# Writing a table of bias rows to DRAM in 21 small transfers, one at a time, in place of two large ones

## What is computed

```
bias = tab_gr[g6, r6, t5_bucket(dist)]          # first block, 8 heads (NSA)
s = einsum(q, k) * scale + bias
...
logits = logits + bias_table[t5_bucket_2(t - s)] # second block, 12 heads of three kinds
```

## Time and profile before

| | |
|---|---|
| median of three runs | 2925.42 us |
| the profiled execution's own time | 2927.45 us |
| its span (first to last instruction) | 2925.6 us |
| PE busy | 2827.9 us (97%) |
| DVE busy | 1870.2 us (64%) |
| ACT busy | 1250.5 us (43%) |
| POOL busy | 154.5 us (5%) |
| weight blocks (raw<-wstream) | 470, 4.8 us from issue to landing in the median |
| the two writes of bias rows | 2 MB and 3.25 MB, 45.9 and 45.8 us to landing |

### The profile page before, as it was taken

One profiled execution on the slowest core, in us unless ns is written; L12 is line 12 of the kernel. 1 busy time (PEld: TensorE's weight loads), 2 busy tenths in 40 slices (PEclk: granted clock), 3 DMA queues, 4 the chain that ended last, 5 costly groups with the idle time before them and its releaser, 6 DMA issues.

```text
span 2925.6 us, 43772 instructions
## 1 busy us (share of the span) xinstructions
PE 2827.9 (97%) x17530; PEld 2518.4 (86%) x17530; DVE 1870.2 (64%) x1955; ACT 1250.5 (43%) x1159; POOL 154.5 (5%) x125
## 2 busy tenths in 40 slices
PE   7898899999999999999999999999999999999997
PEld 5777788888889988888888999988888888888986
DVE  7554555567755678877777545575555765657576
ACT  4343445653363444544444333343334343434442
POOL 3000000000000001000000000010000000000330
PEclk9999899999999999999999999999999999999999
DMA  6546444445545655555555555555554466555753
GB/s 206 194 160 187 152 148 151 160 173 179 178 158 203 243 200 188 179 185 183 186 186 186 218 185 190 185 190 186 186 185 163 174 208 205 184 194 198 281 211 129
DMA packets 94811, 545.51 MB, mean 186 GB/s; under 512 B 11528, under 2 KB 25992, under 8 KB 34288
## 3 DMA queue, kind: packets, MB, share of 16 engines
q1 hardware_dynamic: 84768, 511.01, 49.4%
q0 software_dynamic: 9936, 32.92, 4.0%
HBM read 519.44 MB, written 24.38 MB: 186 GB/s over the span
## 4 chain that ended last, share of the span: by engine, by line
PE 91%; DVE 3%; DMA 3%; ACT 2%; issue 0%; POOL 0%; DVEq 0%; SPq 0%; ACTq 0%
PE gemm L527 46%; PE gemm L530 23%; PE mix L520 3%; PE mix L522 3%; PE mix L521 3%; DMA raw<-wstream 3%; PE gemm L521 2%; PE gemm L522 2%; PE gemm L520 2%; PE mix L527 1%; PE mix L787 1%; DVE wlo L1407 1%; PE mix L627 1%; PE mix L530 1%; ACT whi L970 0%
## 5 line engine op out<-in xcount | busy, mean ns | idle before, releaser
L527 PE MATMUL gemm<-HX,whi 128*128 128x512 f32 x5728 | 2027.6, 401 | 30.2 <-issue 12.3
L530 PE MATMUL gemm<-HX,wlo 128*128 128x256 f32 x5728 | 1555.1, 282 | 0.0
L970 ACT ACTIVATE whi<-raw 128x2048 fp32r<-128x2048 f32 x470 | 899.3, 1914 | 1416.3 <-DMA raw<-wstream 1413.7
L1407 DVE TENSOR_TENSOR wlo<-raw,whi 128x2048 fp32r<-128x2048 f32 x470 | 1086.0, 2311 | 384.5 <-ACT whi L970 383.7
L527 PEld LDWEIGHTS gemm<-HX,whi 128*128 128x128 f32 x5728 | 1066.6, 189 | 266.8 <-issue 25.3
L530 PEld LDWEIGHTS gemm<-HX,wlo 128*128 128x128 f32 x5728 | 1089.2, 190 | 29.8 <-issue 0.7
L1432 DVE TENSOR_REDUCE arena<-gemm 128x256 f32<-128x512 f32 (+1 forms) x173 | 119.6, 691 | 314.7 <-PE gemm L527 314.6
L520 PE MATMUL mix<-ACTH,whi 128*128 (+1 forms) x528 | 149.7, 284 | 0.0
L522 PE MATMUL mix<-ACTH,wlo 128*128 (+1 forms) x528 | 149.7, 283 | 0.0
L521 PE MATMUL mix<-ACTL,whi 128*128 (+1 forms) x528 | 149.7, 283 | 0.0
L522 PE MATMUL gemm<-OH,wlo 128*128 128x256 f32 x384 | 108.9, 284 | 0.0
(11 more groups left out here) (354 smaller groups left out, 2544.6 us busy)
## 6 DMA issues: line engine op xcount, KB each, us to landing
raw<-wstream SPq DMA_DIRECT2D x470, 1024.0 KB, 4.8
scratch<-gate_scratch POOLq DMA_DIRECT2D x12, 512.0 KB, 5.1
gate_scratch<-scratch SPq DMA_DIRECT2D x32, 128.0 KB, 4.6
GL<-gate_scratch POOLq DMA_DIRECT2D x8, 512.0 KB, 5.3
gate_scratch<-arena SPq DMA_DIRECT2D x32, 128.0 KB, 4.6
bias_scratch<-arena POOLq DMA_DIRECT2D x1, 3328.0 KB, 45.8
btile<-bias_scratch POOLq DMA_DIRECT2D x21, 128.0 KB, 2.4
XT<-xT SPq DMA_DIRECT2D x4, 512.0 KB, 9.2
```

What stands on the lines that cost most here:

```text
L527: return pe.matmul(bank.rearrange("p (c t) -> p c t", c=2), whi[slot][:, w], mx, start=first, stop=last)
L530: return pe.matmul(bank[:, 0:T], wlo[slot][:, w], mh, start=False, stop=False)
L970: f(whi[slot][:, :], raw[slot][:, :], ACT.Copy).then_inc(s["hi_ready"], 1)
L1407: tt(wlo[slot][:, :], raw[slot][:, :], whi[slot][:, :].bitcast(F32), ALU.subtract).then_inc(s["lo_ready"], 1)
```

## The change

The two large writes are replaced by a loop over all 21 rows, ahead of the first read. Each turn issues one transfer that writes one row's first `SEG` = 384 columns 128 times over (196,608 bytes), and waits until it has landed. The waits for the second write go, or count to 21 transfers.

```diff
@@ -405,12 +405,10 @@
             pool.wait_ge(s["bias_evac"], 1)
 
-            def rows_out(a, b):
-                pool.dma_start(bias_d[a:b, :, 0:ROWW], brow[a:b, :].unsqueeze(1).to_broadcast([b - a, P, ROWW])
+            for row in range(N_BROW):
+                pool.dma_start(bias_d[row:row + 1, :, 0:SEG], brow[row:row + 1, 0:SEG].unsqueeze(1).to_broadcast([1, P, SEG])
                                ).then_inc(s["bias_out"], 16)
-
-            rows_out(0, HEADS)
-            pool.wait_ge(s["bias_out"], 16)
+                pool.wait_ge(s["bias_out"], 16 * (row + 1))
 
...
                 bias(h, h)
-                if h == 2:
-                    rows_out(HEADS, N_BROW)
 
...
             pool.wait_ge(s["nsa_logit"], HEADS)
-            pool.wait_ge(s["bias_out"], 32)
             pool.wait_ge(s["f_taps"], N_UP)
...
-            act.wait_ge(s["bias_out"], 32)
+            act.wait_ge(s["bias_out"], 16 * N_BROW)
```

## The result

The changed kernel takes 2897.89 us in the median of four runs (2895.51 to 2898.79), the kernel before in the same series 2925.43 us. The ratio is 0.9907, with a 95% interval of 0.9893 to 0.9921. The forecast was 2936 us, with a range of 2885 to 2966: the time lies in the range, but the sign was wrong.

What follows compares the result with a forecast made beforehand. PE was taken as the bound, with two weight-block stalls worth 39.2 us. A loop of 21 turns at 11.6 us ending at 294.3 us gave +10.2 us: 2937.6, less 2.0 to the median, rounded to 2936 us, range 2885 to 2966.

Steps and rivals of the forecast that it cites:

- What bounds it: PE, busy 97% of the span, stalls twice on weight blocks delayed by the two row writes: 14.0 and 25.2 us.
- C: Time of one turn of POOL's row-write loop (issue, transfer, wait): 11.6 us forecast, 9.7 to 13.5 thought plausible.
- E: End of POOL's loop of 21 row writes, 50.7 + 21 C: forecast at 294.3 us.
- my own lower end of 9.7 us: Shortest turn thought plausible for the loop: 7.6 us of data plus 2.1 us per transfer, nothing added for weight blocks.
- the balance: Net change in kernel time for a late loop, E - 284.1 us: +10.2 us forecast, turning to loss above 11.1 us per turn.
- Rival A: Row-write loop fully hidden before head 0, turn at most 9.4 us: whole 39.2 us won, 2886 us; chance 15%.
- The gain when hidden: Both PE stalls and their slow clock vanish if the loop ends by about 249 us: 39.2 us won.
- the slow clock's 6.6 us: Cost of PE's granted clock of 0.52 behind the two stalls: 2.6 and 4.0 us.
- The delayed blocks: Weight blocks during the loop: a few stall PE for 1 or 2 us, vanishing in the wait for head 0's bias.
- My tolerance of 13.2 us: Time a weight block may take to land: three blocks of 5.8 us less 1.9 and 2.3 us of preparation.
- rival B: Row-write loop late but cheap, turn 9.5 to 10.8 us: 7 to 34 us won, 2891 to 2918 us; chance 17%.
- Where the source is shared: Row writes' source in SBUF: four neighbouring rows share a place giving 26 GB/s, so a row's data take 7.6 us.

Runs made afterwards that it cites:

- the 512 columns: The changed kernel with all 512 columns of each row written instead of 384: 2937.56 against 2924.64 us for the kernel before, ratio 1.0039.
- the floor: The changed kernel with only row 0 written and read by every head, so another output: 2890.62 against 2923.49 us for the kernel before, ratio 0.9879.
- far against near rows: The changed kernel with two row writes in flight, from distant partitions (2893.26 us) or in plain order (2908.50 us), both against 2924.64 us for the kernel before.

## Why the prediction was wrong

**What bounds it: right.** Both stalls were weight blocks that waited for row data in the engines. Without the row writes they are gone (the run with one row), and with all row writes issued at once they become one of 49 us.

**The turn: the step that failed.** I took C = 7.6 + 2.1 + 1.9 = 11.6 us; it is 9.25. The term of 1.9 us, "part of the second [block] goes to the turn", was charged as if the engines were the limit. The turns of the changed kernel show its true size. Of the 21, seven in which the weight queue moved 0.9 to 1.1 MB, about one block, took 9.0 to 9.2 us. Eight with 1.9 to 2.4 MB, about two blocks, took 9.1 to 9.7. In the mean that is 9.04 and 9.36 us: the second block costs 0.3 us. Two turns that follow each other, from 144.04 to 153.04 us and from there to 162.28, show why (packets, MB, share of 16 engines):

```profile
q0 software_dynamic: 64, 0.20, 70.0%
q1 hardware_dynamic: 128, 0.92, 25.6%
```

```profile
q1 hardware_dynamic: 304, 2.21, 63.9%
q0 software_dynamic: 64, 0.20, 33.9%
```

The same 64 packets of a row hold the engines for 70% or for 34% of the time, and the turn is 9.0 or 9.2 us long. What the weights take is time in which row packets would have waited for their source. I had read from the earlier trace rows that engines take turns at one source, and then charged the turn for the engines. The other two terms were close: 7.6 us at 26 GB/s, and 1.7 in place of 2.1, with what the weights do cost in it. Over 21 turns the error is 21 x 2.35 = 49 us of E, 245 instead of 294. Some 40 of them are the 1.9 us, and they carry the sign: with my own lower end of 9.7 us the balance would have been 30 us in favour. Rival A's condition (C up to 9.4) held, and I had given it 15%.

**The balance: right.** E - 284.1 was tested by the 512 columns (13.4 against 12.9 us, and head 0 at 307.1 against 306.7). Only its use with C = 11.6 was wrong.

**The gain when hidden: too large.** 39.2 us were counted, the floor gives 32.9: of the slow clock's 6.6 us only 3.5 came back, in one profile of each kernel. And the changed kernel doesn't reach the floor.

**The delayed blocks: underrated.** I wrote that stalls in the loop "vanish in the wait for the bias". Since there was no such wait they counted in full: 7 us against the floor. My tolerance of 13.2 us was for blocks of 5.8 us that nothing but `wlo` waits for. It did not hold for the four blocks that are used up in 3 us each (4.1 us), nor for ACT's own work that stands behind a late block (2.9 us). Rival A's 2886 was missed by 12 us, half for the floor and half for this. That the time lies in rival B's range of 2891 to 2918 is luck: B's turn of 9.5 us and more did not occur.

**Where the source is shared: right,** shown by far against near rows, and by the two large writes.

## What to carry to other kernels

What hurt in this kernel was not that a large transfer from a few neighbouring partitions is slow, but that it holds back the weight blocks behind it in the DMA engines. Cut such a transfer up, keep one or two parts in flight, let parts in flight come from distant partitions, and put them where the stream beside it has blocks to spare. When a loop of waits is on trial, find its break-even per turn first, and then ask of each term which resource limits it: the weights on the engines hardly lengthened a transfer whose source was the limit (0.3 us for 1 MB).

## What the runs showed of the hardware

- A write from one source partition keeps many engines at it (8.5 on average, packets of 1.63 us instead of 0.16) and still moves only 26 GB/s. With all waits counted, one row in flight moved 21 GB/s (9.25 us each) and two from distant partitions 39 (10.0 us a pair).
- Four neighbouring source partitions share the 26 GB/s: 8 rows and 13 rows of 262,144 bytes in one transfer each took 46 us to landing, and two near rows 14.3 us against 10.0.
- A weight block issued beside or behind row data lands later: 4.8 us alone, 8.5 in the median with one row in flight, 20 to 32 beside the large writes, 55 to 64 behind 21 at once.
- Small transfers issued without waits were worse than two large ones: 25.8 us slower than before, against 27.5 us faster with one in flight.
